# Two transitions from row normalisation to projection in a hybrid block: a GpSimd split, one cast and the transposes take other places

## What is computed

```
# block 1, layer 0: conformer mixer; layer 1: gated linear attention (GLA)
c = silu(layer_norm(conv(glu))) * silu(z)
h = layer_norm(ALPHA * h + c @ conv_w_out + b, post_ln[0])     # conv_out
u = h @ gla_w_in ; q, k, v, r, a1 = split(u)                    # gla_in
o = rms_norm(gla(q, k, v, gate)) * silu(r)
h = layer_norm(ALPHA * h + o @ gla_w_out, post_ln[1])           # gla_out
# block 2
hn = rms_norm(h) ; z = hn @ w_in ; q, k, v, f, u = split(z)     # attn_in
```

## Time and profile before

| | before |
|---|---|
| median of 3 runs | 2293.61 us (2293.08 to 2295.3) |
| profiled execution, its own time | 2300.83 us |
| profiled execution, its span | 2299.1 us |
| TensorE busy | 2184.4 us, 95% |
| mean granted TensorE clock | 0.980 |
| VectorE, GpSimd, ScalarE busy | 57%, 45%, 35% |

### The profile page before, as it was taken

The page is one execution under the profiler, slowest core; times in us unless marked ns, Lnnn a source line. Parts: engine busy times, 40 slices in busy tenths (PEclk is TensorE's granted clock), DMA queues, the critical chain, the costliest instruction groups (busy, mean ns, idle before and its releaser), DMA issues.

```text
span 2299.1 us, 31376 instructions
## 1 busy us (share of the span) xinstructions
PE 2184.4 (95%) x12100; PEld 1870.5 (81%) x12100; DVE 1305.2 (57%) x1676; ACT 798.3 (35%) x1296; POOL 1031.3 (45%) x704
## 2 busy tenths in 40 slices
PE   7999989899998999989998999989999999999898
PEld 6999967799998888868896668768888888888576
DVE  2899988700039875740005645676666666666553
ACT  3454442112137752210115754322222222222353
POOL 2789941142236646023285531045555555555300
PEclk9999989999999999999999989999999999999899
DMA  4111122211100023211202013111111111112321
GB/s 132 56 37 37 58 70 91 96 53 52 38 19 1 1 74 129 83 56 55 111 1 79 1 56 113 61 37 37 55 53 47 55 55 55 55 52 77 117 74 46
DMA packets 110603, 136.60 MB, mean 59 GB/s; under 512 B 6977, under 2 KB 92609, under 8 KB 110367
## 3 DMA queue, kind: packets, MB, share of 16 engines
q1 hardware_dynamic: 110494, 135.08, 17.8%
HBM read 118.26 MB, written 16.81 MB: 59 GB/s over the span
## 4 chain that ended last, share of the span: by engine, by line
PE 77%; DVE 11%; POOL 4%; ACT 3%; issue 3%; DMA 2%; SPq 0%; POOLq 0%; DVEq 0%; ACTq 0%
PE PS L352 46%; PE PS L2318 17%; PE PS L1704 3%; PE PS L392 2%; POOL side_sum L532 2%; PE PS L1715 1%; PE PS L1744 1%; DVE att L1227 1%; PE PS L381 1%; PE PS L2613 1%; PE PS L1757 1%; DVE arg_b L1218 1%; DVE arg_a L1218 1%; DVE decay L1203 1%; DVE arg_b L1217 1%
## 5 line engine op out<-in xcount | busy, mean ns | idle before, releaser
L2492 DVE TENSOR_TENSOR ff_acc<-ff_acc,PS 128x512 f32<-128x512 f32 x336 | 227.5, 686 | 193.8 <-PE PS L352 192.5
L352 PE MATMUL PS<-xh,wh 128*128 128x352 f32 (+2 forms) x1024 | 321.8, 345 | 9.8 <-DVE xl L447 4.0
L352 PE MATMUL PS<-xl,wh 128*128 128x352 f32 (+2 forms) x1024 | 319.2, 342 | 0.0
L352 PE MATMUL PS<-xh,wl 128*128 128x352 f32 (+2 forms) x1024 | 318.2, 341 | 0.0
L2257 POOL TENSOR_TENSOR xl<-raw,xh 128x512 fp32r<-128x512 f32 x120 | 168.4, 1411 | 144.0 <-ACT xh L2369 144.0
L352 PE MATMUL PS<-wh,xh 128*128 128x256 f32 (+1 forms) x784 | 229.1, 317 | 4.0 <-DVE wl L343 2.8
L352 PE MATMUL PS<-wl,xh 128*128 128x256 f32 (+1 forms) x784 | 228.1, 316 | 0.0
L352 PE MATMUL PS<-wh,xl 128*128 128x256 f32 (+1 forms) x784 | 227.6, 315 | 0.0
L575 DVE SCALAR_TENSOR_TENSOR PS<-glu,conv_vec,PS 128x1040 f32<-128x1040 f32 x184 | 225.8, 1298 | 0.8
L352 PEld LDWEIGHTS PS<-xh,wh 128*128 128x128 f32 x1024 | 192.2, 191 | 22.0 <-issue 5.8
L352 PEld LDWEIGHTS PS<-xl,wh 128*128 128x128 f32 x1024 | 191.9, 190 | 11.5
(11 more groups left out here) (373 smaller groups left out, 4845.6 us busy)
## 6 DMA issues: line engine op xcount, KB each, us to landing
h_rows<-rows SPq DMA_DIRECT2D x24, 512.0 KB, 2.6
rows<-h_rows SPq DMA_DIRECT2D x24, 512.0 KB, 3.2
dn_raw<-in_w_ffn_down_dram SPq DMA_DIRECT2D x22, 512.0 KB, 3.6
raw<-in_gla_w_in_dram SPq DMA_DIRECT2D x10, 1024.0 KB, 5.1
raw<-in_w_ffn_gate_dram SPq DMA_DIRECT2D x20, 512.0 KB, 3.7
raw<-in_w_ffn_up_dram SPq DMA_DIRECT2D x20, 512.0 KB, 4.7
raw<-in_conv_w_in_dram SPq DMA_DIRECT2D x16, 512.0 KB, 4.8
raw<-in_w_in_dram SPq DMA_DIRECT2D x8, 1024.0 KB, 5.5
```

The lines of the kernel that those rows point to most:

```text
L352: last = nc.tensor.matmul(out_of(c, cn), s, x[:, c0:c0 + cn], start=n == 0 and m == 0, stop=n == len(terms) - 1 and m == 2)
L2492: ins = nc.vector.tensor_tensor(x, x, PS[:, 6 + n % 2, :], ALU.add)
```

## The change

Five edits, three in kind.

The GpSimd split of the second unit starts later at both transitions: behind `h1_done` 9 instead of `dense_done` 9, and behind `n5_done` 8 instead of `dense_done` of the last tile. Its work is the same.

ScalarE's high part of row tile t - 2 is moved at the last tile of both: at the first transition ahead of the wait for the last row's variance, at the second behind the last root of the layer norm and ahead of the squares.

Transposes on TensorE are moved between matmuls. At the first, turn(3) goes from behind dense 5 into the middle of dense 6, and turn(7) from ahead of part(1, 0) to behind it. At the second, the products of the first two channel tiles are cut: part(1, first half) is made for k = 0 to 3, then turn(6), then for k = 4 to 7, then turn(7), and the second half of channel tile 0 is made in two pieces of 256 columns, with the wait for the last low part between them. The order of the three products within a k changes from (wh xh, wh xl, wl xh) to (wh xh, wl xh, wh xl).

```diff
@@ conv_out_tensor
+                of = lambda k: (xh[:, k, cols], xl[:, k, cols]), lambda k: of_slots(CO_SLOTS, k), 2 * (t % 3)
+                if t == 6:
+                    dense_split(*of, range(4))
+                    turn(3)
+                    dense_split(*of, range(4, KT)).then_inc(dense_done, 1)
+                else:
+                    dense_split(*of).then_inc(dense_done, 1)
-                for done in {1: (), 2: (), 3: (0,), 4: (1,), 5: (2, 3)}.get(t, (t - 2,)):
+                for done in {1: (), 2: (), 3: (0,), 4: (1,), 5: (2,)}.get(t, (t - 2,)):
                     turn(done)
...
             part(0, 0)
-            turn(7)
             pe.wait_ge(dense_left, 9)
             part(1, 0)
+            turn(7)
             pe.wait_ge(part_lo, H1 + 7)
             part(0, 1)
@@ conv_out_scalar
             for t, (c0, n) in enumerate(TILES):
+                if t == len(TILES) - 1:
+                    high(t - 2)
                 act.wait_ge(row_var, t + 1)
                 nc.scalar.activation(STD[0:n, :], VAR[0:n, :], ACT.Sqrt, bias=LN_EPS).then_inc(row_std, 1)
-                if t >= 2:
+                if 2 <= t < len(TILES) - 1:
                     high(t - 2)
@@ gla_in_pool
             pool.wait_ge(dense_done, 9)
+            pool.wait_ge(h1_done, 9)
             split_unit(pool, U_GQK + 1, QK_SLOTS[1])
-            pool.wait_ge(h1_done, 9)
@@ gla_out_tensor
-            part = lambda t, c: channel_part(wh[1], wl[1], t, CHUNKS2, c, 2 * t)
+            def part(t, c0, cn, ks=range(KT)):
+                cols, b0 = slice(t * P, (t + 1) * P), c0 % HALF
+                for k in ks:
+                    for m, (h, x) in enumerate(((wh, xh), (wl, xh), (wh, xl))):
+                        ins = nc.tensor.matmul(PS[:, 2 * t + c0 // HALF, b0:b0 + cn], h[1][:, k, cols], x[:, k, c0:c0 + cn],
+                                               start=k == 0 and m == 0, stop=k == KT - 1 and m == 2)
+                return ins
+
             pe.wait_ge(unit_ready, U_AQK + 1)
             pe.wait_ge(part_lo, N5 + 4)
             pe.wait_ge(dense_left, Y5 + 7)
-            part(0, 0)
+            part(0, 0, HALF)
+            pe.wait_ge(dense_left, Y5 + 8)
+            part(1, 0, HALF, range(4))
             turn(NX - 2)
-            pe.wait_ge(dense_left, Y5 + 8)
-            part(1, 0)
+            part(1, 0, HALF, range(4, KT))
             turn(NX - 1)
+            part(0, HALF, 2 * P)
             pe.wait_ge(part_lo, N5 + NX)
-            part(0, 1).then_inc(in6_tile, 1)
-            part(1, 1).then_inc(in6_tile, 1)
+            part(0, HALF + 2 * P, 2 * P).then_inc(in6_tile, 1)
+            part(1, HALF, HALF).then_inc(in6_tile, 1)
@@ gla_out_scalar
                 nc.scalar.activation(STD, VAR, ACT.Sqrt, bias=LN_EPS).then_inc(row_std, 1)
+                if j == NX - 1:
+                    high(j - 2)
                 act.wait_ge(h2_done, j + 1)
...
-                if j >= 2:
+                if 2 <= j < NX - 1:
                     high(j - 2)
@@ gla_out_pool
-            pool.wait_ge(dense_done, Y5 + NX)
+            pool.wait_ge(n5_done, NX)
             split_unit(pool, U_AQK + 1, 0)
```

More of the change, by code:

```diff
@@ L343, in split_unit_fast, with products @@
             nc.vector.tensor_tensor(wl[slot][:], buf[:], wh[slot][:].bitcast(F32), ALU.subtract).then_inc(unit_ready, 1)
-        def products(terms, chunks, out_of):
+        def products(terms, chunks, out_of, ks=None):
             for n, (sh, sl, mh, ml) in enumerate(terms):
+                if ks is not None and n not in ks:
+                    continue
                 for m, (s, x) in enumerate(((sh, mh), (sh, ml), (sl, mh))):
@@ L371, in token_tile, with dense_split @@
                              for k in range(KT)], [(0, UNIT)], lambda c, cn: PS[:, bank, 0:cn])
-        def dense_split(act_of, w_of, bank):
-            return products([act_of(k) + w_of(k) for k in range(KT)], [(0, HALF), (HALF, HALF)], lambda c, cn: PS[:, bank + c, :])
+        def dense_split(act_of, w_of, bank, ks=None):
+            return products([act_of(k) + w_of(k) for k in range(KT)], [(0, HALF), (HALF, HALF)], lambda c, cn: PS[:, bank + c, :], ks)
         def dense_stage(act_of, w_of, bank, first=False, last=False):
@@ L767, in conv_out_tensor @@
                 cols = slice(c0, c0 + P)
-                dense_split(lambda k: (xh[:, k, cols], xl[:, k, cols]), lambda k: of_slots(CO_SLOTS, k), 2 * (t % 3)).then_inc(dense_done, 1)
-                for done in {1: (), 2: (), 3: (0,), 4: (1,), 5: (2, 3)}.get(t, (t - 2,)):
+                of = lambda k: (xh[:, k, cols], xl[:, k, cols]), lambda k: of_slots(CO_SLOTS, k), 2 * (t % 3)
[6 more added lines that the diff above has]
+                for done in {1: (), 2: (), 3: (0,), 4: (1,), 5: (2,)}.get(t, (t - 2,)):
                     turn(done)
```

## The result

| | before | after |
|---|---|---|
| median, first timing | 2293.70 us (4 runs) | 2273.14 us (4 runs, 2268.63 to 2275.97) |
| ratio, 95% interval | | 0.9907 [0.989, 0.9925] |
| mean of the runs with a clock on record, all timings | 2295.9 us (31 runs) | 2273.1 us (10 runs) |
| profiled execution, time and span | 2300.83, 2299.1 us | 2274.58, 2272.7 us |
| mean granted clock in it | 0.980 | 0.988 |

The changed kernel is faster by 20.6 us by the first medians, and its 2273.1 us lies in the range of 2264 to 2277. Over all runs the means differ by 22.8 us, but 19 of the 31 runs of before come from a chip on which the changed kernel did not run. Both savings are 2 to 4 us short of the predicted 24.6.

What follows compares the result with a forecast made beforehand. TensorE was taken as the bound, through its waits and slow running at two transitions. Savings of 11.6 and 13.0 us sum to 24.6, taken from the median: 2269 us, 1.07% less; range 2264 to 2277 for 8 in 10.

Steps and rivals of the forecast that it cites:

- turn(4) for low(3): First transition: a new TensorE stall of 0.5 us (0.7 with lost overlap) replaces the one of 2.56.
- First transition: Term for the first transition: 2.05 us from turn(3) plus 9.5 around turn(7), together 11.6 us saved.
- Moving turn(3): First transition, turn(3) into the middle of dense 6: gain of 2.05 us.
- slow matmuls: First transition, 48 matmuls behind the 6.6 us wait: 9.44 us against 7.54 at usual pace, so 1.90 us saved.
- The margin of turn(7): First transition: turn(7) may start at 456.6, TensorE's two parts end at 456.8; no idle, 0.2 us to spare.
- Second transition: Term for the second transition: idle 6.54 and 2.35 us, slow transposes and slow matmuls go, less 0.1; 13.0 us saved.
- The cut chunk: Second transition: cutting half a channel tile into two pieces of 256 columns costs 0.1 us.
- Splits at no cost: Both transitions: the later GpSimd splits are ready before TensorE wants them, with 11.9 and 9.4 us of cover.
- The lock: Rival: the late split, now beside low(7) and low(6), holds those up instead; gain 16 us, 2277 us; chance 5%.
- L798 was slow because of GpSimd: Rival said otherwise: L798 is long for another reason, chains stay 3.1 us longer, 4.2 less gain, 2273 us; chance 3%.
- The clock did not stay low in the denser stretches: Rival said otherwise: denser stretches are refused the full clock, kernel slower, example 2299 us; chance 3%.
- Given back later: Rival: behind the transitions, shifted low-clock time costs 3 us, or 5 to 12 with a late load; 2274 to 2281; chance 10%.
- the last one: Final step: the profiled execution stands 7.2 us above the median; the same 24.6 us saving is taken from the median, giving 2269.

Runs made afterwards that it cites:

- the late split alone: The kernel of before with only its two GpSimd splits started later, all else unchanged; 12 runs, median 2292.2 us, ratio to before 0.998.
- old order on TensorE: The changed kernel with TensorE's order put back at both transitions, keeping the later splits and early high parts; one run, 2283.7 us.
- split at row_var: The changed kernel with both GpSimd splits released earlier, by the last row's variance, 4.1 us into the row chain; one run, 2282.1 us.
- first and of the second transition alone: Two kernels, each before with only one transition's three hunks: first, median 2283.1 us, ratio 0.9938; second, median 2283.7 us, ratio 0.9947.

## Why the prediction was right

**What bounds it.** This was right in each place: all four waits of TensorE are gone, and the one that was to take the first's place, turn(4) for low(3), is 0.75 us, where 0.5 was said.

**First transition, 11.6 forecast, 11.1 in the trace.** Moving turn(3) gave 1.85 instead of 2.05. The pace of 352 columns was taken over 103 matmuls of which some had 336 and came out as 0.157; it is 7.77 / 48 = 0.162, so the slow matmuls had cost 1.67, not 1.90. The margin of turn(7) held: low(6) is done at 458.51 and the part ahead ends at 459.02, which leaves 0.37 us behind the 0.14 from low to turn, where 0.2 was forecast.

**Second transition, 13.0 forecast, 13.0 in the trace.** No wait opened; low(6), ended at 998.98, leaves 0.5 us to turn(7), 0.36 behind the same 0.14, as forecast (0.3). The cut chunk cost 0.1 us, as taken from the rows: the last 72 matmuls, 48 of them cut ones, took 11.25 us, against 11.15 for 48 uncut ones of the same columns in all. Of its parts, the late split alone cuts the wait of turn(6) from 6.5 to 3.4, the early high cuts it to 0.9 (old order on TensorE), and the cut products hide that and the 2.36 behind turn(7). The changed order of the three products within a k was in no run by itself; 24 matmuls of 512 columns in the old order (old order on TensorE) take 5.57 us and 36 in the new one 8.36, which is 0.232 each in both.

**Splits at no cost.** This was right: U_GQK + 1 was ready at 464.1 and U_AQK + 1 at 1002.3, and TensorE waited for neither.

**The rivals.** The lock did not move: `low` beside the split kept 1.22 us. L798 was slow because of GpSimd: shown by the late splits alone and the split at row_var. The clock did not stay low in the denser stretches: 1.00 in both. Given back later: 0.45 us in the trace between the transitions, and up to some 5 us is not excluded by the times (24.1 against 21.4, with an error of 1.2).

**The sum against the time.** The trace bears out 24.1 of the 24.6 us; the 0.5 that is missing is mainly a gain of 1.85 taken as 2.05 and slow matmuls of 1.67 taken as 1.90. The times give less, 20.6 and 20.5 us by medians. The step that no run bears out is the last one: it took the saving read in one execution, 7.2 us above the median, and applied it whole to the median. That forecast was 4 us off, and it hit because its range was 13 us wide. Why the step came out short is open. Giving back accounts for the 0.45 us above. That the slow stretches of 6.9 us were a peculiarity of the execution read is not borne out: they came again in the traces of the first and of the second transition alone. Most of what that execution had above the median stands elsewhere, behind the second transition, where it took 1265.6 us and the middle one of the eleven traces 1260.1.

## What to carry to other kernels

Read a slow VectorE operation with two SBUF operands beside GpSimd as a wait: subtract the hold of the other engine from its duration before costing a move, and move the GpSimd work past the last operation with two SBUF operands, if its own reader has the slack. Where a turn waits for cast and subtraction (2.3 us), put independent matmuls of at least that length between two turns; half a product will do, since an accumulation may be interrupted by transposes into other banks (36 and 12 matmuls around turn(6) took 8.36 and 2.81 us, the usual 0.23 each). Price waits and the slow clock behind them as separate terms, and before a gain under 1% is read off medians, time both kernels some ten times on the same chip and put the time beside the mean granted clock.

## What the runs showed of the hardware

One kernel spread over 16.7 us (0.7%), and most of it went with the mean granted clock, 0.980 to 0.989. Waits of TensorE of 6.5 us were followed by a stretch at 1.2 GHz in every trace read that had one, and it cost the same each time (at the first transition 2.7 us beyond the wait). Waits of 2.5 to 3.5 us were followed by one in some executions and not in others, so the cost of one is the wait plus 0 to 3 us. And a blocked operation of either engine shows as a long one, GpSimd's too (2.96 for 1.90, 5.44 for 4.61).
